# Five stage borders of a hybrid decoder step: stores, dilated pieces, one gate unit, waits per k-block, and a load in four parts

## The chip, the cores and the metric

The kernel runs on one core of a Trainium2 chip. The metric is the device time of one execution in microseconds; the figure for a kernel is the median of its runs. The profile is one execution recorded by the hardware profiler. Its engines are PE (TensorE, matmuls), PEld (its weight loads), DVE (VectorE), ACT (ScalarE), POOL (GpSimd) and SP (the sync engine, here only a queue that issues transfers). All of them run at once and are ordered by semaphores.

## The reference

One layer of a decoder for a prompt (256 tokens) and a sample group (8 sequences of 8 new tokens with 2048 past ones), 320 columns together. All data is 32-bit.

```python
h = rmsnorm(x, g_pre_mix)                              # 2048 channels
q_f, k_f, v_f, f_logit, q_d, k_d, v_d = split(h @ w_in)  # 8 fox heads, 3 x 4 dilated heads, 128 wide
o_fox = softmax(q k / sqrt(128) + forget_bias) v       # prompt: causal; sample: paged cache of 2048 keys
o_dil = three dilated windows (128,1) (512,4) (2048,16), merged by their softmax sums
g_fox, g_dil = split(sigmoid(h @ w_gate + b_gate))     # 2 x 2048 gates
m = (g_fox * (o_fox @ w_o_fox) + g_dil * (o_dil @ w_o_dil)) @ w_out
x1 = x + rmsnorm(m, g_post_mix)
y = x1 + rmsnorm(swiglu(rmsnorm(x1, g_pre_ffn), w_gate_up, w_down), g_post_ffn)   # 5632 wide
# also returned: y, new keys, values and log-forgets, and the shifted window caches
```

## The kernel before

**Units and panels.** Every dense product is made of units of 128 output columns. The weights of two units make a panel (2 MB) that SP loads into one of two slots of `raw`. ScalarE copies a unit's half into `w_hi` in a rounded format (`split_hi`, L1269; in the gate stage `gate_split`, L1369), VectorE computes the remainder `w_lo` (L1592, L1803), and TensorE runs three matmuls for each of the 16 k-blocks: `w_hi` by `act_hi`, `w_hi` by `act_lo`, `w_lo` by `act_hi`. Units are numbered: 0 to 23 fox queries, keys and values; 24 to 59 the dilated ones; 60 to 91 gates; 92 (`U_O`) to 107 the two attention output projections, twelve k-blocks each; 108 (`U_OUT`) to 123 the output projection; 124 on up and gate of the FFN, and 212 to 275 the down projection in four quarters of 11 k-blocks. Panel p holds units 2p and 2p + 1. Each engine runs its own program in written order; counting semaphores tie them: `unit_done` (TensorE has finished a unit), `hi_done`/`lo_done` (its weights are split), `acc_free` (its result has been taken from PSUM, unit u gives the value u + 3).

**Projections (to 585 us).** TensorE runs units 0 to 65. A natural-layout copy of keys goes through `k_stage` (two slots; `nat_rows`, L1313 on) and out by Pool's stores (L602, L603). ScalarE waits for `k_out` before it overwrites a slot. At units 10 to 14 the forget bias of the caches is computed (`fbx`), which Pool stores to `scratch_fb` (L595). Between half units, the attention of the prompt runs in pieces: half unit t = 2u or 2u + 1 starts a head's piece if `FOX_AT` or `DIL_AT` (L372) says so. A dilated head begins with its scores at t0; probabilities are normalised by VectorE at t0 + 1, transposed by TensorE at t0 + 3 and copied by ScalarE (`d_pt`, L1353), multiplied with the values at t0 + 5, and the result copied by VectorE (`pd_free`, L1782).

**Gates.** The gates of a unit are evicted by ScalarE (`gate_out`, L1361) into `gst`, two slots, and stored by SP to `scratch_gates` (`store_gates`, L483), since they are needed only at units 92 to 107. `gate_out(u)` waits until store u - 2 has landed. SP's program alternates stores and panels: ahead of panel p it stores the gates up to `due` (L494). From unit 66 on (`U_DEC`) all panels use slot 0 of `raw`, because slot 1's place holds value tiles.

**Attention of the samples (588 to 1285 us).** Nine blocks, one for each sequence and one more: block q works on the keys of sequence q and the values of sequence q - 1, tile by tile in 24 steps. Keys come through a ring of three buffers (`kraw`, L653) and values through one of four (`vraw`, L690), 512 KB a tile, both issued by Pool when TensorE has read a buffer. Before its first new key Pool waits for `pd_free` of all dilated heads, clears `fb` (L679) and loads the bias (L697). `GATE_UNITS` (L345) says how many gate units each block interleaves: (2, 3, 3, 3, 4, 3, 3, 3, 2), units 66 to 91. After the last block TensorE turns the last output (`turn_out`), VectorE takes it (`take_out`), ScalarE and VectorE split it into `o_hi` and `o_lo` (L1470, L1942; semaphore `o_sp`), and unit 92 starts.

**Output projections.** For each unit 92 to 107 VectorE first splits the unit after next (`step`), then multiplies with the gates `gl` and merges (`merge_trip`, L1945 on) into a k-block of `act_hi` and `act_lo`. TensorE waits for the last merge (`pe.wait_ge(acc_free, U_OUT + 2)`, L1192) before it starts unit 108.

**FFN and tail.** `x1`, the residual, was stored to scratch. Beside the FFN Pool copies the window caches (`copy_windows`, 22 pieces in 18 units, paced by `unit_done`), and between the copies of the seventh and the eighth sequence it loads `x1T` (2.5 MB, L774). VectorE needs it only at the very end.

Of the kernel before, what the change touches and what calls it, by code (L numbers as in the profile page):

```python
# [143 lines left out]
def build(nc, I, O, scratch):  # L144
    with ExitStack() as ctx:
# [199 lines left out]
        GATE_UNITS = (2, 3, 3, 3, 4, 3, 3, 3, 2)  # L345
# [26 lines left out]
        FOX_AT, DIL_AT = 50, (88, 94, 120, 126)  # L372
# [78 lines left out]
        def _(sp):  # L451
# [34 lines left out]
            for p in range(U_O // 2):  # L486
# [7 lines left out]
                due = 2 * p - (4 if p <= U_DEC // 2 else 2)  # L494
# [40 lines left out]
        def _(pool):  # L535
# [43 lines left out]
            for h in range(HG):  # L579
# [12 lines left out]
                                    bass.IndirectOffsetOnAxis(ap=tcol[:, 0:1], axis=0)).then_inc(lfp_ld, 16)  # L592
            pool.wait_ge(fbx_ok, 1)
# [3 lines left out]
            kp = O["fox_k_prompt"][0, 0].rearrange("(t p) h d -> p t (h d)", p=P)  # L597
            ks = O["fox_k_sample"][0].rearrange("b t h d -> (b t) (h d)")
            for i in range(4):
# [3 lines left out]
                pool.dma_start(ks[:, 256 * i:256 * i + 256], k_stage[0:NS, s, 2, :]).then_inc(k_out[s], 16)  # L603
# [119 lines left out]
            pool.wait_ge(g_st[1], 16 * KT)  # L723
# [35 lines left out]
            def copy_windows(b):  # L759
# [14 lines left out]
            pool.dma_start(x1T[:], scratch["x1T"].rearrange("k p t -> p k t")).then_inc(x1_ld, 16)  # L774
            copy_windows(DB - 1)
# [14 lines left out]
        def _(pe):  # L790
# [392 lines left out]
            turn_out(DB - 1)  # L1183


            pe.wait_ge(acc_free, U_O + 2)
# [941 lines left out]
```

## Time and profile before

| | us |
|---|---|
| median of 3 runs | 2504.24 |
| lowest, highest | 2496.71, 2505.09 |
| profiled execution, span (first to last instruction) | 2501.8 |
| TensorE busy in it | 2347.5 (94%) |
| VectorE, ScalarE, Pool busy | 1066.3, 811.7, 465.1 |
| transfers in it | 585.84 MB |

The page gives the profiled execution's span and no time around it; the median stands 2.4 us over that span. The busy shares are means over stages with different limits, so the stages have to be read one by one: in the timeline, a number in brackets at the end of a row is the time that the engine sat idle before the instruction, with what ended the wait.

### The profile page before, as it was taken

Reading aid. Unit: us, or ns where it says so; the run is one execution under the profiler, and the core shown is the slowest. Engines: PE = TensorE matmul, PEld = TensorE weight load, DVE = VectorE, ACT = ScalarE, POOL = GpSimd, SP = SyncE. Lnnn points to the kernel's source line nnn. Section 1 sums busy time; section 2 is a strip of 40 time slices with the busy share of each in tenths; the row PEclk is TensorE's granted clock in tenths of the full one; section 3 lists DMA queues with packets and bytes.
Section 4 is the critical chain, followed back from the end, with each engine's and each line's share of the span. In section 5 each row is a group of like instructions: output and inputs, shape, how many; then the busy total and the mean of one; then the engine's idle time right before and its main releaser. Section 6 shows DMA issues by size and latency. Waiting matters only on the chain.

```text
span 2501.8 us, 45253 instructions
## 1 busy us (share of the span) xinstructions
PE 2347.5 (94%) x18252; PEld 2140.3 (86%) x18252; DVE 1066.3 (43%) x1433; ACT 811.7 (32%) x982; POOL 465.1 (19%) x874
## 2 busy tenths in 40 slices
PE   7999999997899998999989896999999999999997
PEld 6999999996666666766659895999999999999997
DVE  6443443433333332333326436444444444444445
ACT  3223333332333333333312234232332332333234
POOL 2010000101333333333211232111111111111111
PEclk8999999998999999999989998999999999999998
DMA  8554344535899999999876544667676767688873
GB/s 250 159 153 150 119 144 130 185 125 172 283 348 354 338 314 348 349 343 320 318 242 193 177 157 146 226 230 238 230 247 220 256 217 247 221 276 280 289 272 101
DMA packets 340076, 585.84 MB, mean 234 GB/s; under 512 B 20575, under 2 KB 283043, under 8 KB 336255
## 3 DMA queue, kind: packets, MB, share of 16 engines
q0 software_dynamic: 70704, 309.02, 35.2%
q1 hardware_dynamic: 269232, 274.86, 34.7%
q8 instruction: 99, 1.62, 0.3%
q14 instruction: 41, 0.34, 0.0%
HBM read 564.06 MB, written 109.39 MB: 269 GB/s over the span
## 4 chain that ended last, share of the span: by engine, by line
PE 77%; DMA 11%; issue 4%; DVE 4%; ACT 2%; POOL 1%; POOLq 0%; SPq 0%; DVEq 0%; ACTq 0%
PE ps L798 14%; PE ps L800 14%; PE ps L799 14%; DMA kraw<-in_cache_fox_k 6%; PE ps L836 5%; PE ps L838 5%; PE ps L837 5%; PE ps L1025 3%; DMA kraw<-in_cache_win_k 2%; PE ps L1030 2%; PE ps L1050 2%; PE ps L1110 1%; PE ps L1014 1%; PE ps L1016 1%; PE ps L1015 1%
## 5 line engine op out<-in xcount | busy, mean ns | idle before, releaser
L1592 DVE TENSOR_TENSOR w_lo<-raw,w_hi 128x2048 fp32r<-128x2048 f32 (+2 forms) x250 | 525.6, 2102 | 813.5 <-ACT w_hi L1269 813.5
L1269 ACT ACTIVATE w_hi<-raw 128x2048 fp32r<-128x2048 f32 (+2 forms) x250 | 439.3, 1757 | 1058.0 <-PE ps L800 770.5
L798 PE MATMUL ps<-act_hi,w_hi 128*128 128x320 f32 x1632 | 507.1, 311 | 12.3 <-DVE act_lo L1956 6.6
L799 PE MATMUL ps<-act_lo,w_hi 128*128 128x320 f32 x1632 | 506.7, 310 | 0.0
L800 PE MATMUL ps<-act_hi,w_lo 128*128 128x320 f32 x1632 | 506.5, 310 | 0.0
L836 PE MATMUL ps<-act_hi,w_hi 128*128 128x320 f32 x1024 | 322.9, 315 | 3.2 <-DVE v_stage L1700 3.2
L798 PEld LDWEIGHTS ps<-act_hi,w_hi 128*128 128x128 f32 x1632 | 308.2, 189 | 12.8 <-DVE act_lo L1956 6.9
L838 PE MATMUL ps<-act_hi,w_lo 128*128 128x320 f32 x1024 | 316.9, 309 | 0.0
L837 PE MATMUL ps<-act_lo,w_hi 128*128 128x320 f32 x1024 | 316.7, 309 | 0.0
L799 PEld LDWEIGHTS ps<-act_lo,w_hi 128*128 128x128 f32 x1632 | 308.3, 189 | 0.0
L800 PEld LDWEIGHTS ps<-act_hi,w_lo 128*128 128x128 f32 x1632 | 308.2, 189 | 0.0
L1838 DVE COPY kT<-ps 128x512 f32<-128x512 f32 x176 | 121.5, 690 | 231.3 <-PE ps L1030 230.8
L1402 ACT ACTIVATE kT<-ps 128x512 f32<-128x512 f32 x184 | 109.5, 595 | 312.1 <-PE ps L1025 311.9
L836 PEld LDWEIGHTS ps<-act_hi,w_hi 128*128 128x128 f32 x1024 | 192.6, 188 | 4.3 <-DVE w_lo L1592 3.5
L837 PEld LDWEIGHTS ps<-act_lo,w_hi 128*128 128x128 f32 x1024 | 192.6, 188 | 0.1
L838 PEld LDWEIGHTS ps<-act_hi,w_lo 128*128 128x128 f32 x1024 | 192.3, 188 | 0.0
L1025 PEld LDWEIGHTS ps<-ident,kraw 128*128 128x128 f32 x736 | 80.1, 144 | 108.9 <-DMA kraw<-in_cache_fox_k 49.7
L767 POOL TENSOR_TENSOR tick<-tick 1x1 f32<-1x1 f32 x144 | 28.2, 196 | 723.5 <-PE ps L800 714.6
L1025 PE MATMUL ps<-ident,kraw 128*128 128x128 f32 x736 | 123.7, 292 | 33.8 <-DMA kraw<-in_cache_fox_k 26.3
L1014 PE MATMUL ps<-act_hi,w_hi 128*128 128x320 f32 x416 | 149.6, 360 | 0.0
L1015 PE MATMUL ps<-act_lo,w_hi 128*128 128x320 f32 x416 | 130.2, 313 | 0.0
L1016 PE MATMUL ps<-act_hi,w_lo 128*128 128x320 f32 x416 | 130.1, 313 | 0.0
(368 smaller groups left out, 3735.7 us busy)
## 6 DMA issues: line engine op xcount, KB each, us to landing
raw<-in_w_gate_up SPq DMA_DIRECT2D x88, 1024.0 KB, 6.4
kraw<-in_cache_fox_k POOLq DMA_DIRECT2D x128, 512.0 KB, 6.8
vraw<-in_cache_fox_v POOLq DMA_DIRECT2D x128, 512.0 KB, 7.6
raw<-in_w_in SPq DMA_DIRECT2D x60, 1024.0 KB, 7.8
raw<-in_w_gate SPq DMA_DIRECT2D x32, 1024.0 KB, 15.0
raw<-in_w_down SPq DMA_DIRECT2D x32, 1024.0 KB, 5.8
out_win_k_sample<-in_cache_win_k POOLq DMA_DIRECT2D x64, 510.0 KB, 5.9
out_win_v_sample<-in_cache_win_v POOLq DMA_DIRECT2D x64, 510.0 KB, 3.9
```

What stands on the lines that cost most here:

```text
L798: pe.matmul(ps[:, bk_, 0:T], w_hi[:, slot, k, :], xh[:, x_k, :], start=(k == k0), stop=False)
L799: pe.matmul(ps[:, bk_, 0:T], w_hi[:, slot, k, :], xl[:, x_k, :], start=False, stop=False)
L800: mm = pe.matmul(ps[:, bk_, 0:T], w_lo[:, slot, k, :], xh[:, x_k, :], start=False, stop=(k == k1 - 1))
L836: pe.matmul(acc, w_hi[:, u % 2, k, :], act_hi[:, k, :], start=(k == 0), stop=False)
L837: pe.matmul(acc, w_hi[:, u % 2, k, :], act_lo[:, k, :], start=False, stop=False)
L838: mm = pe.matmul(acc, w_lo[:, u % 2, k, :], act_hi[:, k, :], start=False, stop=(k == KT - 1))
L1014: pe.matmul(acc, w_hi[:, u % 2, k, :], act_hi[:, k, :], start=(k == 0), stop=False)
L1015: pe.matmul(acc, w_hi[:, u % 2, k, :], act_lo[:, k, :], start=False, stop=False)
L1016: mm = pe.matmul(acc, w_lo[:, u % 2, k, :], act_hi[:, k, :], start=False, stop=(k == KT - 1))
L1025: mm = pe.transpose(ps[:, 2, P * j:P * j + P], kraw[:, n % KRING, P * j:P * j + P], ident[:])
L1269: act.activation(w_hi[:, slot, 0:kt, :], raw[:, pslot, 0:kt, P * slot:P * slot + P], ACT.Copy).then_inc(hi_done, 1)
L1592: dve.tensor_tensor(w_lo[:, slot, 0:kt, :], raw[:, pslot, 0:kt, P * half:P * half + P], w_hi[:, slot, 0:kt, :].bitcast(F32), ALU.subtract) ...
```

## The change

Five places are edited.

1. *Key stores.* Pool stores the first two pairs of fox keys ahead of the wait for `fbx` and the stores of `scratch_fb`, and the other two behind them.
2. *Start of the attention.* The last two dilated heads begin a half unit earlier (`DIL_AT` 119 and 125). SP stores gates 62 and 63 ahead of panel 33 instead of behind it.
3. *End of the attention.* The last block interleaves one gate unit instead of two; unit 91 runs behind `turn_out`. ScalarE and VectorE split unit 92 first, take and split the last output, then evict unit 91 and split unit 93. SP issues panel 47 before the store of unit 91, and Pool waits for that store only before the last four loads of `gl`.
4. *Unit 108.* TensorE starts it when its weights are split and waits for the two last merges only at k-blocks 14 and 15. VectorE merges unit 107 before it splits unit 109.
5. *x1.* The load becomes four of 640 KB, placed before the second, 7th, 12th and 17th piece of the last sequence's window copies.

```diff
-        GATE_UNITS = (2, 3, 3, 3, 4, 3, 3, 3, 2)
+        GATE_UNITS = (2, 3, 3, 3, 4, 3, 3, 3, 1)
-        FOX_AT, DIL_AT = 50, (88, 94, 120, 126)
+        FOX_AT, DIL_AT = 50, (88, 94, 119, 125)
...
-                due = 2 * p - (4 if p <= U_DEC // 2 else 2)
+                due = 2 * p - (4 if p < U_DEC // 2 else 2)
...
-            store_gates(U_O - 2, U_O)
+            store_gates(U_O - 2, U_O - 1)
             sp.wait_ge(pv_done, DB * KPG)
             load_panel(1, U_O, [(0, wof[:, :, 256:512]), (8, wod[:, :, 256:512])])
+            store_gates(U_O - 1, U_O)
...
+            store_fox_keys(0)
+            store_fox_keys(1)
             pool.wait_ge(fbx_ok, 1)
             for b in range(DB):
                 pool.dma_start(fbd[b].rearrange("h (g t) -> g h t", t=P), fbx[NPG * b:NPG * b + NPG]).then_inc(fb_st, 16)
+            store_fox_keys(2)
+            store_fox_keys(3)
...
-            pool.wait_ge(g_st[1], 16 * KT)
+            pool.wait_ge(g_st[1], 16 * KT - 16)
...
-            with pool.Fori(0, KT // 4) as i:
+            with pool.Fori(0, KT // 4 - 1) as i:
                 for k in range(4):
-                    pool.wait_ge(acc_free, i * 4 + (U_O + k - 1))
-                    pool.dma_start(gl[:, k], halves[bass.ds(i * 4 + k, 1)].rearrange("e p o t -> p (e o) t")).then_inc(g_ld[k], 16)
+                    load_gates(i, k)
+            pool.wait_ge(g_st[1], 16 * KT)
+            for k in range(4):
+                load_gates(KT // 4 - 1, k)
...
+                    if m % 5 == 1 and m // 5 < quarters:
+                        part = slice(4 * (m // 5), 4 * (m // 5) + 4)
+                        pool.dma_start(x1T[:, part, :], scratch["x1T"][part].rearrange("k p t -> p k t")).then_inc(x1_ld, 16)
...
-            pool.dma_start(x1T[:], scratch["x1T"].rearrange("k p t -> p k t")).then_inc(x1_ld, 16)
-            copy_windows(DB - 1)
+            copy_windows(DB - 1, 4)
...
             turn_out(DB - 1)
-            pe.wait_ge(acc_free, U_O + 2)
+            dense(U_O - 1, 0, KT)
+            pe.wait_ge(acc_free, U_O + 1)
             pe.wait_ge(o_sp, 1)
...
-            pe.wait_ge(acc_free, U_OUT + 2)
-            for e in range(KT):
+            pe.wait_ge(lo_done, U_OUT + 1)
+            for k in range(KT):
+                if k >= KT - 2:
+                    pe.wait_ge(acc_free, U_O + k + 3)
+                acc = ps[:, 0, 0:T]
+                pe.matmul(acc, w_hi[:, 0, k, :], act_hi[:, k, :], start=(k == 0), stop=False)
+                pe.matmul(acc, w_hi[:, 0, k, :], act_lo[:, k, :], start=False, stop=False)
+                mm = pe.matmul(acc, w_lo[:, 0, k, :], act_hi[:, k, :], start=False, stop=(k == KT - 1))
+            mm.then_inc(unit_done, 1)
+            for e in range(1, KT):
...
+            def last_gate():
+                for late in range(2):
+                    gate_split(U_O, late)
+                act.wait_ge(o_ev, DB)
+                act.activation(o_hi[:, :, SEQ:T], o32[:, :, SEQ:T], ACT.Copy).then_inc(os_h, 1)
+                gate_out(U_O - 1)
+                for late in range(2):
+                    gate_split(U_O + 1, late)
...
-            for n in range(6):
-                gates_after(DB + 1, n)
+            for late in range(2):
+                gate_split(U_O, late)
             take_out(DB - 1)
             dve.wait_ge(os_h, 4)
             dve.tensor_tensor(o_lo[:, :, SEQ:T], o32[:, :, SEQ:T], o_hi[:, :, SEQ:T].bitcast(F32), ALU.subtract).then_inc(o_sp, 1)
+            for late in range(2):
+                gate_split(U_O + 1, late)
...
-                    step(i * 4 + (U_O + k), k, KT if last and k >= 2 else KO)
+                    if last and k == 3:
+                        dve.wait_ge(unit_done, U_OUT)
+                    else:
+                        step(i * 4 + (U_O + k), k, KT if last and k >= 2 else KO)
...
             merge_trip(KT // 4 - 1, True)
+            split_lo(1, 0, U_OUT + 1)
...
-            dve.wait_ge(x1_ld, 16)
+            dve.wait_ge(x1_ld, 64)
```

What stands in a row on the engines, at three of the places. In these rows a semaphore behind "waits" is one that the instruction waits for.

SP at the end of the projections, before: the panels 31 to 33 and the gate stores.

```order
L467 DMA raw<-in_w_gate 128x8x256 [waits lo_done]
L467 DMA raw<-in_w_gate 128x8x256
L483 DMA scratch_gates<-gst 128x320 [waits acc_free] x2
L467 DMA raw<-in_w_gate 128x8x256 [waits lo_done]
L467 DMA raw<-in_w_gate 128x8x256
L483 DMA scratch_gates<-gst 128x320 [waits acc_free] x4
```

And after:

```order
L467 DMA raw<-in_w_gate 128x8x256 [waits lo_done]
L467 DMA raw<-in_w_gate 128x8x256
L483 DMA scratch_gates<-gst 128x320 [waits acc_free] x4
L467 DMA raw<-in_w_gate 128x8x256 [waits lo_done]
L467 DMA raw<-in_w_gate 128x8x256
L483 DMA scratch_gates<-gst 128x320 [waits acc_free] x2
```

The stores of gates 62 and 63 moved from behind panel 33, the second pair of loads, to ahead of it.

ScalarE at the same place, before: the gate outputs (gst) of units 63, 64 and 65, the splits (w_hi) behind them, and the copy of the last dilated probabilities (d_pt).

```order
L1361 ACTIVATE gst<-ps,cols 128x320 [waits unit_done]
L1269 ACTIVATE w_hi<-raw 128x2048 [waits raw_ld0]
L1361 ACTIVATE gst<-ps,cols 128x320 [waits unit_done,g_st0,out_lf]
L1269 ACTIVATE w_hi<-raw 128x2048 [waits raw_ld0]
L1353 ACTIVATE d_pt_103<-ps 128x1152 [waits pd_t]
L1361 ACTIVATE gst<-ps,cols 128x320 [waits unit_done,g_st1,out_lf]
```

And after:

```order
L1387 ACTIVATE gst<-ps,cols 128x320 [waits unit_done]
L1295 ACTIVATE w_hi<-raw 128x2048 [waits raw_ld0]
L1379 ACTIVATE d_pt_103<-ps 128x1152 [waits pd_t]
L1387 ACTIVATE gst<-ps,cols 128x320 [waits unit_done,g_st0,out_lf]
L1295 ACTIVATE w_hi<-raw 128x2048 [waits raw_ld0]
L1387 ACTIVATE gst<-ps,cols 128x320 [waits unit_done,g_st1,out_lf]
```

The copy moved ahead of the gate output of unit 64 and of the split of unit 66.

TensorE behind the last attention block, before: the last turn of the output, then unit 92.

```order
L1144 MATMUL ps<-ident,of 128x128 [waits od_ok,of_ok]
L1144 MATMUL ps<-ident,of 128x128
L1146 MATMUL ps<-sel,od 128x16 x2
L1188 UNCONDITIONAL_BRANCH [waits o_sp,acc_free]
L1188 ISA
L798 MATMUL ps<-o_hi,w_hi 128x320 [waits acc_free,lo_done]
```

And after:

```order
L1161 MATMUL ps<-ident,of 128x128 [waits od_ok,of_ok]
L1161 MATMUL ps<-ident,of 128x128
L1163 MATMUL ps<-sel,od 128x16 x2
L853 MATMUL ps<-act_hi,w_hi 128x320 [waits acc_free,lo_done]
L854 MATMUL ps<-act_lo,w_hi 128x320
```

The 48 matmuls of gate unit 91 stand between the turn and the wait for `o_sp`.

VectorE at the last merge, before: the split of unit 109 (w_lo), then the merge of unit 107.

```order
L1592 TENSOR_TENSOR w_lo<-raw,w_hi 128x2048 [waits hi_done,unit_done]
L1952 TENSOR_TENSOR mtmp<-ps,gl 128x320 [waits g_ld3]
L1953 TENSOR_TENSOR mtmp<-ps,gl 128x320
L1954 TENSOR_TENSOR mtmp<-mtmp 128x320 [waits vchain]
L1955 CAST act_hi<-mtmp 128x320 [waits vchain]
L1956 TENSOR_TENSOR act_lo<-mtmp,act_hi 128x320 [waits vchain]
```

And after:

```order
L1991 TENSOR_TENSOR mtmp<-ps,gl 128x320 [waits g_ld3,unit_done]
L1992 TENSOR_TENSOR mtmp<-ps,gl 128x320
L1993 TENSOR_TENSOR mtmp<-mtmp 128x320 [waits vchain]
L1994 CAST act_hi<-mtmp 128x320 [waits vchain]
L1995 TENSOR_TENSOR act_lo<-mtmp,act_hi 128x320 [waits vchain]
L1626 TENSOR_TENSOR w_lo<-raw,w_hi 128x2048 [waits hi_done]
```

The split moved behind the merge.

## Rows read from the trace of the kernel before

**Rows 1.** The page, part 4: shares of the chain that ended last, by engine.

```profile
PE 77%; DMA 11%; issue 4%; DVE 4%; ACT 2%; POOL 1%; POOLq 0%; SPq 0%; DVEq 0%; ACTq 0%
```

**Rows 2.** Timeline, key stores: start, duration, engine, line, operation, [idle before <- releaser].

```profile
157.20 4.28 POOL L595 DMA_DIRECT2D scratch_fb<-fbx  x8 [68.91 <-DVE fbx L1744]
...
164.77 0.38 ACT L1325 ACTIVATE k_stage<-ps 128x256 f32<-128x256 f32 x1 [12.32 <-DMA out_fox_k_sample<-k_stage]
...
170.58 0.38 PE L836 MATMUL ps<-act_hi,w_hi 128*128 128x320 f32 x1 [3.22 <-DVE v_stage L1700]
```

**Rows 3.** Timeline, start of the samples' attention, all engines.

```profile
571.36 1.02 SPq L467 DMA_DIRECT2D raw<-in_w_gate  x2
572.42 13.13 SPq L483 DMA_DIRECT2D scratch_gates<-gst  x4
...
581.43 0.53 ACT L1361 ACTIVATE gst<-ps,cols 128x320 f32<-128x320 f32 x1 [12.50 <-DMA scratch_gates<-gst]
...
584.83 0.48 PE L991 MATMUL ps<-d_pt,dV 128*128 128x256 f32 x1 [3.95 <-ACT d_pt L1353]
...
588.13 1.04 PE L1025 MATMUL ps<-ident,kraw 128*128 128x128 f32 x4
...
589.31 0.42 DVE L1782 COPY o<-ps 128x256 f32<-128x256 f32 x1
...
605.53 0.69 PE L1025 MATMUL ps<-ident,kraw 128*128 128x128 f32 x2 [8.31 <-DMA kraw<-in_cache_fox_k]
```

**Rows 4.** Timeline, end of the attention.

```profile
1269.49 1.05 POOL L690 DMA_DIRECT2D vraw<-in_cache_win_v  x2 [2.10 <-PE ps L1116]
...
1275.87 1.05 PE L1116 MATMUL ps<-vraw,pg 128*16 128x256 f32 x8 [2.74 <-DMA vraw<-in_cache_win_v]
...
1291.15 0.61 PE L798 MATMUL ps<-o_hi,w_hi 128*128 128x320 f32 x1 [5.42 <-DVE o_lo L1942]
```

**Rows 5.** Timeline, between the two output projections.

```profile
1386.12 2.29 DVE L1592 TENSOR_TENSOR w_lo<-raw,w_hi 128x2048 fp32r<-128x2048 f32 x1 [0.77 <-ACT w_hi L1269]
...
1390.68 0.64 PE L798 MATMUL ps<-act_hi,w_hi 128*128 128x320 f32 x1 [6.61 <-DVE act_lo L1956]
...
1399.75 1.92 ACT L1269 ACTIVATE w_hi<-raw 128x2048 fp32r<-128x2048 f32 x1 [13.74 <-PE ps L800]
```

**Rows 6.** Timeline, down projection at the load of x1T.

```profile
2363.52 2.64 ACT L1269 ACTIVATE w_hi<-raw 128x1408 fp32r<-128x1408 f32 x2 [9.14 <-DMA raw<-in_w_down]
...
2367.09 0.60 PE L798 MATMUL ps<-q_hi,w_hi 128*128 128x320 f32 x1 [5.89 <-DVE yacc L2057]
...
2373.95 1.38 ACT L1269 ACTIVATE w_hi<-raw 128x1408 fp32r<-128x1408 f32 x1 [7.79 <-PE ps L800]
```

**Rows 7.** Stretches: from:to, length, busy (x) of each engine, PEclk, DMA share, GB/s.

```profile
571.40:579.60 8.20, 7.76 (x56) 7.50 (x55) 1.15 (x3) 0.00 (x0) 0.00 (x0) 1.00 0.90 288
...
592.30:605.50 13.20, 4.26 (x53) 3.18 (x53) 2.46 (x10) 0.60 (x1) 3.96 (x7) 0.76 1.04 253
...
1391.00:1400.00 9.00, 9.00 (x52) 9.00 (x52) 0.00 (x0) 0.25 (x1) 1.08 (x1) 0.80 1.07 365
...
1560.00:1800.00 240.00, 240.00 (x1639) 240.00 (x1638) 109.88 (x102) 73.10 (x52) 27.71 (x76) 1.00 0.69 231
```

**Rows 8.** The page, part 6: transfers, KB each, median us from issue to landing.

```profile
raw<-in_w_down SPq DMA_DIRECT2D x32, 384.0 KB, 7.2
...
x1T<-scratch_x1T POOLq DMA_DIRECT2D x1, 2560.0 KB, 13.6
```

**Rows 9.** The chain in order of time: start, us, what.

```profile
813.59 1.71 POOL fb L697 x3
...
893.08 1.71 POOL fb L697 x3
...
980.99 1.71 POOL fb L697 x3
...
2345.71 17.78 DMA raw<-in_w_down
```

More of the change, by code:

```diff
@@ L592, in _, with store_fox_keys @@
                                     bass.IndirectOffsetOnAxis(ap=tcol[:, 0:1], axis=0)).then_inc(lfp_ld, 16)
-            pool.wait_ge(fbx_ok, 1)
-            for b in range(DB):
-                pool.dma_start(fbd[b].rearrange("h (g t) -> g h t", t=P), fbx[NPG * b:NPG * b + NPG]).then_inc(fb_st, 16)
             kp = O["fox_k_prompt"][0, 0].rearrange("(t p) h d -> p t (h d)", p=P)
             ks = O["fox_k_sample"][0].rearrange("b t h d -> (b t) (h d)")
-            for i in range(4):
+            def store_fox_keys(i):
                 s = i % 2
@@ L603, in _ @@
                 pool.dma_start(ks[:, 256 * i:256 * i + 256], k_stage[0:NS, s, 2, :]).then_inc(k_out[s], 16)
+            store_fox_keys(0)
+            store_fox_keys(1)
+            pool.wait_ge(fbx_ok, 1)
+            for b in range(DB):
+                pool.dma_start(fbd[b].rearrange("h (g t) -> g h t", t=P), fbx[NPG * b:NPG * b + NPG]).then_inc(fb_st, 16)
+            store_fox_keys(2)
+            store_fox_keys(3)
             pool.wait_ge(nat_ev, 2 * HF)
@@ L726, in _, with load_gates @@
             halves = gsc.rearrange("(o e) p t -> e p o t", o=2)
-            with pool.Fori(0, KT // 4) as i:
+            def load_gates(i, k):
+                pool.wait_ge(acc_free, i * 4 + (U_O + k - 1))
+                pool.dma_start(gl[:, k], halves[bass.ds(i * 4 + k, 1)].rearrange("e p o t -> p (e o) t")).then_inc(g_ld[k], 16)
+            with pool.Fori(0, KT // 4 - 1) as i:
                 for k in range(4):
-                    pool.wait_ge(acc_free, i * 4 + (U_O + k - 1))
-                    pool.dma_start(gl[:, k], halves[bass.ds(i * 4 + k, 1)].rearrange("e p o t -> p (e o) t")).then_inc(g_ld[k], 16)
+                    load_gates(i, k)
+            pool.wait_ge(g_st[1], 16 * KT)
+            for k in range(4):
+                load_gates(KT // 4 - 1, k)
             pool.wait_ge(acc_free, U_OUT + 2)
@@ L757, in _, with copy_windows @@
             pool.wait_ge(tick_ok, 1)
-            def copy_windows(b):
+            def copy_windows(b, quarters=0):
                 for m, (g, x, n, rows) in enumerate(pieces):
                     unit = m * 18 // len(pieces)
+                    if m % 5 == 1 and m // 5 < quarters:
+                        part = slice(4 * (m // 5), 4 * (m // 5) + 4)
+                        pool.dma_start(x1T[:, part, :], scratch["x1T"][part].rearrange("k p t -> p k t")).then_inc(x1_ld, 16)
                     if m == 0 or unit != (m - 1) * 18 // len(pieces):
@@ L1466, in _ @@
             sequence(DB, None, DB - 1)
-            for n in range(6):
-                gates_after(DB + 1, n)
-            act.wait_ge(o_ev, DB)
-            act.activation(o_hi[:, :, SEQ:T], o32[:, :, SEQ:T], ACT.Copy).then_inc(os_h, 1)
+            gate_out(U_O - 2)
+            last_gate()
             ahead[:] = [panel_landed(U_O // 2) - loads(U_O) - 32, panel_landed(U_O // 2 + 1) - loads(U_O) - 32]
@@ L1937, in _ @@
             sequence(DB, None, DB - 1)
-            for n in range(6):
-                gates_after(DB + 1, n)
+            for late in range(2):
+                gate_split(U_O, late)
             take_out(DB - 1)
```

## The prediction

> **What bounds the kernel now.** I read the page first: the chain that ended last is TensorE for 77% of the span and transfers for 11% [rows 1]. A change can win only where TensorE waits on that chain, or where its clock is down because it waited. So I went through TensorE's timeline for waits, and took clock and transfers from the stretches view. The attention (606 to 1284 us) is largely paced by key and value transfers, and the change leaves its inner order alone. Outside it there are few long waits, and the change addresses five places: 3.22 us before 170.58 [rows 2], 3.95 and 8.31 at the start of the attention [rows 3], 5.42 at its end [rows 4], 6.61 between the two output projections [rows 5], 5.89 in the last quarter of the down projection [rows 6].
>
> A unit is one 128-column block of weights, 16 k-blocks of three matmuls. In a stretch without waits 1639 matmuls take 240 us [rows 7], 0.1464 us each, so a unit takes 7.03 us, and a down unit (11 k-blocks) 4.83. After the waits of 6.61 and 5.89 us the engine is slow for a while: the unit from 1390.68 to 1399.75 took 9.07 us instead of 7.03 [rows 5], and the granted clock of that stretch is 0.80 of 2.4 GHz [rows 7], a mix of 1.2 and 2.4. The down unit from 2367.09 to 2373.95 took 6.86 instead of 4.83 [rows 6]. So a long wait costs its length and 2.0 us more. The 3.22 us wait started no such phase: its first matmul takes 0.38 us, against 0.60 to 0.64 after the long ones [rows 2, 5, 6].
>
> **Key stores first (border 1).** Pool waits for fbx, issues the eight stores of scratch_fb at 157.20 for 4.28 us, and only then the key stores. ScalarE wants to overwrite k_stage, sits 12.32 us until a key store has landed, the next weight split behind it is late, and TensorE waits 3.22 us [rows 2]. With the first two pairs of key stores ahead of the wait for fbx they land before ScalarE asks. The scratch_fb stores keep their time; what now waits behind them is the third pair, whose tile is written only then. Gain 3.2 us. Nothing is late next: the weight panels are not waited for here. The bounds are 0 and 3.2; I take 3.2, since the named releaser is the very thing moved.
>
> **Dilated pieces and gate stores (border 2).** Now the sync queue issues panel 33 at 571.36 and behind its wait the stores of gate outputs 62 to 65. ScalarE may not overwrite gst before store 62 has landed and sits 12.50 us, to 581.43. Its copy of the last dilated probabilities comes after that, so TensorE waits 3.95 us, from 580.9, and does the last product slowly, to 588.13. VectorE copies the result at 589.31, which lets Pool clear fb, load it and fetch the next keys, and TensorE waits for these to 605.53 [rows 3].
> After the change stores 62 and 63 go out before panel 33, as soon as their outputs are written, and the gst wait goes. Late next is panel 33 itself. From 571.4 to 579.6 the transfers move 8.2 x 288 GB/s = 2.36 MB [rows 7], the panel's 2.10 and some gate outputs, so it lands by 579.6. ScalarE's split of unit 66 (1.9 us) ends at 581.5, VectorE's (2.3 us) at 583.9, and in VectorE's order the copy that frees Pool comes then: 584.3 instead of 589.7, **5.4 us** earlier. If the keys land as long after it as now, the gain is 5.4. The other bound is panel 34, issued when VectorE has split unit 67, now just ahead of that copy at 589.4. TensorE's unit 65 will end at about 582 (580.9, and about 1.5 for the product at full clock, done inside it); 0.5 us of eviction and 1.9 and 2.3 of splits put the issue at 587.1, only **2.3 us** earlier. Now fb and keys start 3 us behind the panel, then they start with it, and the engines are full from 592.3 to 605.5 at only 253 GB/s [rows 7]. If that whole backlog ends last, the gain is 2.3. I take the middle, 3.9 us, as no row is nearer to one end.
> The Trainium skill, page "DMA: Bandwidth & Descriptors", section "Queues, rings and completion order", says that a DMA engine takes turns between its queues packet by packet. By that rule Pool's key load shares the engines with the panel until the panel is through, the lower bound holds, and the sum comes out 1.6 us less. The trace shows only the case with the panel ahead and does not settle it.
>
> **A gate unit behind the attention (border 3).** Now TensorE waits 5.42 us behind the last attention output [rows 4] and starts the output projection slowly, 2.0 us more by the price above. Unit 91 (7.03 us) takes this place and hides the eviction of unit 90, the splits of unit 92 and the copy and low part of o, that 5.4 us in all. Its own eviction and the splits of unit 93 (about 4 us) hide under unit 92 (12 k-blocks, 5.3 us). At the border alone that is 5.42 + 2.0 - 7.03 = 0.4 us. The rest is how much shorter the last attention block gets without the unit, between 0 (value transfers pace it) and 7.03 (TensorE paces it). There are four value buffers, and a load starts when its buffer is read; the pair issued at 1269.49 is used from 1275.87 [rows 4]: 6.4 us, or 1.6 us a value tile, while TensorE's work per tile is 32/24 of a k-block (0.44 us) and 0.5 for the values (1.05 at half clock), 1.1 us. So much of the block is paced by transfers and saves nothing. TensorE paces its end, from 1275.87 on, at half clock at first [rows 4]: some 3 of its gate steps go there, 2.5 us; I put another 1.5 on the rest. I take 4.0, so border 3 gives **4.4 us**, with 0.4 and 7.4 as ends.
>
> **Waits per k-block (border 4).** Now VectorE first splits unit 109 (1386.12, 2.29 us) and then merges the last output unit, 2.3 us to 1390.68, and TensorE waits 6.61 us, from 1384.07 [rows 5]. After the change VectorE merges first, to about 1386.5, and TensorE works through 14 k-blocks of unit 108 (6.2 us, to 1390.2) before it needs the last two. The split of unit 109 moves behind the merge and ends at 1388.9, before unit 108 does at 1391.1, so the removed wait has no successor. Unit 108 ends at 1391.1 instead of 1399.75: **8.6 us**. Pool's load of xT starts with the merge and meets panel 56: 4.7 MB together, 12.9 us at the 365 GB/s of [rows 7], so by 1400; the first split of that panel is due after unit 110, at 1405. The bounds are 6.6 (the slow phase stays) and 8.7.
>
> **x1 in four parts (border 5).** Now x1T, 2.5 MB, goes out just ahead of a down panel, which is then 17.78 us on its way from 2345.71 [rows 9]; ScalarE waits 9.14 us for it, to 2363.52, and TensorE 5.89 [rows 6]. TensorE's wait began at 2361.2, one unit after 2356.4, when the panel was due: it had 10.7 us. Its second part usually takes 7.2 us, and a quarter of x1T's 13.6 is 3.4 [rows 8]: 10.6 us if the quarter stood wholly ahead. It goes out behind the panel instead, and the others 4, 9 and 13 units later, so no wait. Gain 5.89 + 2.0 = **7.9 us**, the lower end 3 (one quarter still makes a panel a few us late). VectorE's wait for all four parts comes tens of us after the last.
>
> **The sum.** 3.2 + 3.9 + 4.4 + 8.6 + 7.9 = **28.0 us**. The profiled execution has a span of 2501.8 us and the median is 2504.24; the 2.4 us between them the change does not touch. 2504.24 - 28.0 = **2476.2 us**, 1.1% less. The lower ends of the five terms give 12.3, the upper ones 32.6.
>
> **Rivals.**
> (a) *The transfers hold borders 2 and 3.* The keys give 2.3 us and the last block nothing. For it: full engines from 592 to 605 [rows 7], a wait for values at 1275.87 [rows 4]. Against it: from there on TensorE is busy without a wait. 2504.2 - (3.2 + 2.3 + 0.4 + 8.6 + 7.9) = 2481.8.
> (b) *The x1 stall moves and does not go.* A quarter meets window pieces and a panel four times; 10.6 against 10.7 us leaves no room [rows 8]. One late panel brings back up to 7.9: 2484.1.
> (c) *The attention slips against its own panels*, slower than before. Its blocks start at 813.59, 893.08 and 980.99 [rows 9]: 79.5 us with three gate units, 87.9 with four. The change starts the attention with panel 34 and the keys at once. If that puts each later panel in front of the keys, and each of the six later blocks with three units takes what the one with four does, that is 6 x 8.4 = 50 us: 2526. It decides the sign from 4.7 us a block on. Against it: every block is re-ordered by its own waits, and the order inside is the same.
> (d) *The last block is TensorE's after all*, and the keys give 5.4: 1.5 + 3.0 more, 2471.7.
>
> **Chances.** Forecast 0.61, (a) 0.14, (b) 0.08, (c) 0.04, (d) 0.08, and 0.05 for most terms at their lower ends at once (12.3 us, 2491.9). A measurement of this kernel can tell about 0.5%, 12.5 us, from no change; the runs of before lie within 8.4. Forecast, (a), (b) and (d) all stay under 2491.7, which is the border of faster; the lower ends together are "same". The range goes from 2468 (below (d) by half the spread of the runs) to 2488 (above (b) by as much). Faster 0.91, same 0.05, slower 0.04.
>
> **What the profile after would show.** Border 1: no wait of ScalarE for out_fox_k_sample, none of TensorE over 1 us near 170. Border 2: gate output 64 near 570 in place of 581.43, ScalarE's next wait on raw, and the wait for keys ending near 598. Border 3: matmuls of act_hi between the last turn and the output projection, and no wait over 1 us there. Border 4: no wait of 6.61, and unit 108 in 7.0 us at clock 1.00. Border 5: four x1T loads, no wait of ScalarE on in_w_down over 1 us. I am wrong if a wait over 3 us stands at one of the last three borders, or if the attention, from its first waited key to its last value, is 5 us longer than the terms allow.

## The result, and the profile after

| | before | changed |
|---|---|---|
| median, us | 2504.66 (4 runs) | 2481.32 (4 runs, 2477.52 to 2485.61) |
| ratio, 95% interval | | 0.9910 (0.9897 to 0.9923) |
| five more runs of the changed kernel (e5 below) | 2504.69 (11 runs) | 2480.54, ratio 0.9902 (0.9889 to 0.9916) |
| span of the profiled execution | 2501.8 | 2482.7 |

The change takes 23.3 us off the median, 24.2 in the second comparison; the forecast was 28.0. By the intervals of the ratios it is 19 to 26 us and 21 to 28, so the 28.0 lies at or just beyond their upper ends. The time lies inside the predicted range (2468 to 2488) and 5.1 us above the predicted value. The two profiled spans differ by 19.1 only; 3.3 us of what is missing there is a stall that the profile of after shown here caught and other executions don't have (border 5 below). One run of e2 below took 5137.37 us; it counts in no ratio, and without it that median is 2502.55.

The chain that ended last, by engine, in the page of after:

```profile
PE 79%; DMA 11%; issue 4%; DVE 3%; ACT 2%; POOL 1%; POOLq 0%; SPq 0%; DVEq 0%; ACTq 0%
```

TensorE's share has risen by 2 points against [rows 1] and the transfers' 11% have not moved. That is a first hint, and no more: what was recovered is TensorE's waits at borders, and little of what transfers hold.

**Border 1.** Timeline of after, Pool (start, duration, engine, line, operation, [idle before <- releaser]):

```profile
131.07 0.79 POOL L601 DMA_DIRECT2D out_fox_k_prompt<-k_stage  x1 [42.57 <-ACT k_stage L1352]
...
146.03 0.73 POOL L601 DMA_DIRECT2D out_fox_k_prompt<-k_stage  x1 [13.62 <-ACT k_stage L1352]
...
157.41 2.68 POOL L608 DMA_DIRECT2D scratch_fb<-fbx  x5 [10.11 <-DVE fbx L1778]
```

The two key stores now go out 11 and 26 us ahead of the bias stores, which keep their time (157.20 in [rows 2]). ScalarE's wait for a key store and TensorE's 3.22 us are gone.

**Border 2.** Timeline of after, sync queue, ScalarE, VectorE and TensorE at the start of the attention:

```profile
563.90 0.33 SPq L483 DMA_DIRECT2D scratch_gates<-gst  x1
568.10 1.02 SPq L467 DMA_DIRECT2D raw<-in_w_gate  x2
...
570.10 0.53 ACT L1387 ACTIVATE gst<-ps,cols 128x320 f32<-128x320 f32 x1 [2.52 <-PE ps L855]
577.43 1.92 ACT L1295 ACTIVATE w_hi<-raw 128x2048 fp32r<-128x2048 f32 x1 [6.80 <-DMA raw<-in_w_gate]
...
581.66 0.42 DVE L1816 COPY o<-ps 128x256 f32<-128x256 f32 x1
...
584.30 1.02 SPq L467 DMA_DIRECT2D raw<-in_w_gate  x2
...
600.94 1.11 PE L1042 MATMUL ps<-ident,kraw 128*128 128x128 f32 x4 [7.31 <-DMA kraw<-in_cache_fox_k]
```

To be read against [rows 3]: gate output 64 comes at 570.10 instead of 581.43, then ScalarE waits for panel 33, as forecast. VectorE's copy, which frees Pool, comes at 581.66 instead of 589.31, 7.65 us earlier; 3.26 of these are border 1's, so 4.4 are left. But the keys arrive at 600.94 instead of 605.53, 4.59 earlier, so 1.3 without border 1. Panel 34 goes out at 584.30, in the middle of it. The chain in order of time (start, us from issue to landing) has the load of the first waited keys, in before, in after and in e12 below, where panel 34 goes out behind it:

```profile
595.34 10.15 DMA kraw<-in_cache_fox_k
```

```profile
587.67 13.23 DMA kraw<-in_cache_fox_k
```

```profile
588.72 9.09 DMA kraw<-in_cache_fox_k
```

The load goes out 4.4 us earlier in after (border 1 apart) and takes 3.1 us longer.

**Border 3.** TensorE and VectorE at the end of the attention, after:

```profile
1275.45 0.62 PE L1133 MATMUL ps<-vraw,pg 128*16 128x256 f32 x8 [1.26 <-DMA vraw<-in_cache_win_v]
...
1279.45 0.39 PE L853 MATMUL ps<-act_hi,w_hi 128*128 128x320 f32 x1
...
1283.48 0.96 DVE L1976 TENSOR_TENSOR o_lo<-o,o_hi 128x768 fp32r<-128x768 f32 x1 [0.91 <-ACT o_hi L1466]
```

Unit 91 starts at 1279.45 right behind the turn, and `o_lo` is written at 1283.48 beside it. The wait of 5.42 us in [rows 4] has no successor.

**Border 4.** VectorE's split of unit 109 in the timeline of after, and the stretch in which TensorE runs unit 108 (from:to, length, busy time and instructions of PE, PEld, DVE, ACT, POOL, PEclk, DMA share, GB/s):

```profile
1386.51 2.29 DVE L1626 TENSOR_TENSOR w_lo<-raw,w_hi 128x2048 fp32r<-128x2048 f32 x1 [3.39 <-ACT w_hi L1295]
```

```profile
1375.00:1386.00 11.00, 11.00 (x77) 11.00 (x76) 7.91 (x12) 3.43 (x2) 1.16 (x1) 1.00 0.48 149
```

TensorE is busy for the whole 11 us, at the full clock, where [rows 5] and the third stretch of [rows 7] had a wait of 6.61 and a clock of 0.80.

**Border 5.** Pool's four loads, ScalarE and TensorE, after:

```profile
2334.12 0.82 POOL L779 DMA_DIRECT2D x1T<-scratch_x1T  x1
...
2352.98 0.80 POOL L779 DMA_DIRECT2D x1T<-scratch_x1T  x1
...
2372.34 0.80 POOL L779 DMA_DIRECT2D x1T<-scratch_x1T  x1
...
2384.75 2.79 ACT L1295 ACTIVATE w_hi<-raw 128x1408 fp32r<-128x1408 f32 x2 [6.88 <-DMA raw<-in_w_down]
...
2388.42 0.38 PE L815 MATMUL ps<-a_hi,w_hi 128*128 128x320 f32 x1 [2.29 <-DVE yacc L2097]
```

Three of the four loads are shown; the fourth goes out at 2394.23. The first two pass unnoticed. Behind the third, ScalarE waits 6.88 us for a down panel and TensorE 2.29, where [rows 6] had 9.14 and 5.89.

### The profile page after: what moved, and what is told of

Its sections match the earlier page's. It is cut to its first block, busy times and chain, and to the rows that moved or that the text cites. A ratio compares the mean times of both kernels' runs of the same rounds, so it can differ in the third digit from the quotient of the medians.

```text
span 2482.7 us, 45242 instructions
## 1 busy us (share of the span) xinstructions
PE 2348.4 (95%) x18252; PEld 2140.8 (86%) x18252; DVE 1065.7 (43%) x1433; ACT 812.7 (33%) x982; POOL 468.8 (19%) x877
## 4 chain that ended last, share of the span: by engine, by line
PE 79%; DMA 11%; issue 4%; DVE 3%; ACT 2%; POOL 1%; POOLq 0%; SPq 0%; DVEq 0%; ACTq 0%
PE ps L815 14%; PE ps L817 14%; PE ps L816 14%; DMA kraw<-in_cache_fox_k 6%; PE ps L853 6%; PE ps L855 6%; PE ps L854 6%; PE ps L1042 3%; PE ps L1047 2%; DMA kraw<-in_cache_win_k 2%; PE ps L1067 2%; PE ps L1127 1%; PE ps L1031 1%; PE ps L1033 1%; PE ps L1032 1%
```

## The experiments

The theory from this comparison: borders 1 and 4 give what they should; border 2's lead is cut by panel 34 and then given back inside the attention, because transfers and not TensorE set its length; border 5 keeps a stall in some executions. In the expectations this theory is T, and T2 in its later form. The rivals: the forecast's terms all hold and the trace of after is a poor sample; or the attention absorbs whatever is done at its ends. Each edit was run alone on the kernel before or taken out of the changed one, and each suspected cause was changed by itself.

**e1: border 2 alone.**

```diff
-        FOX_AT, DIL_AT = 50, (88, 94, 120, 126)
+        FOX_AT, DIL_AT = 50, (88, 94, 119, 125)
...
-                due = 2 * p - (4 if p <= U_DEC // 2 else 2)
+                due = 2 * p - (4 if p < U_DEC // 2 else 2)
```

> The kernel before with the second edit alone (dilated pieces a half unit earlier, gates 62 and 63 stored ahead of panel 33). Theory T (each term is what the trace of after shows at its border, and the missing gain went there): the wait for the first keys ends only 1.3 to 1.6 us earlier, since their load now shares the transfer engines with panel 34, and the median falls by 1.5 us. Rival N (the trace of after is one execution among many; the forecast's term holds): 3.9 us. Rival A (the attention takes back any earlier start, because its blocks run against transfers that the start doesn't move): the keys 1.5 or more earlier, but no gain is left at the last value of the attention, 0 us. T and A differ in the lead at block 8: more than 1 us by T, none by A.

Measured: 2502.13 against 2505.90, ratio 0.9984 (0.9969 to 0.9999), which is 0.3 to 7.8 us: T's 1.5 and N's 3.9 are both inside, rival A's 0 just outside. In the traces (table below) the keys come 2.0 us earlier than in before, and block 8 begins no earlier (879.33 against 879.02), as rival A has it; one pair of traces can't settle it.

**e2: border 3 alone** (the hunks of the third edit; the first of them):

```diff
-        GATE_UNITS = (2, 3, 3, 3, 4, 3, 3, 3, 2)
+        GATE_UNITS = (2, 3, 3, 3, 4, 3, 3, 3, 1)
...
             turn_out(DB - 1)
+            dense(U_O - 1, 0, KT)
```

> The kernel before with the third edit alone (one gate unit moved behind the attention). Theory T: the last block 4.5 us shorter and no wait over 1 us behind it, 5.3 us in all. Rival N: the forecast's 4.4 us. Rival A (the last block is shorter in after only because the attention arrived there with another lead): the block is shorter by 2 us or less here and the edit gives 1 to 3 us.

Measured: 2502.80 against 2505.90, ratio 0.9994 (0.9980 to 1.0008), at most 5.0 us. T's 5.3 us is just outside; N's 4.4 and A's 1 to 3 are both inside.

**e3: border 5 alone.**

```diff
-            pool.dma_start(x1T[:], scratch["x1T"].rearrange("k p t -> p k t")).then_inc(x1_ld, 16)
-            copy_windows(DB - 1)
+            copy_windows(DB - 1, 4)
...
```

> The kernel before with the fifth edit alone (x1T in four parts). Theory T: the third part meets a panel and window pieces, ScalarE waits some 7 us for that panel and TensorE about 2.3, so 5.3 us of the forecast's 7.9 are left. Rival N: no wait of TensorE over 1 us in the last quarter of the down projection, 7.9 us.

Measured: 2500.20 against 2505.90, ratio 0.9979 (0.9967 to 0.9991), 2.3 to 8.3 us. The trace has no wait of TensorE over 1 us in the last quarter: for this execution rival N is right.

**e4: the four parts at the tail**, on the changed kernel, behind the last window copy:

```diff
-            copy_windows(DB - 1, 4)
+            copy_windows(DB - 1)
...
+            for q, u in enumerate((269, 271, 273, 274)):
+                part = slice(4 * q, 4 * q + 4)
+                pool.wait_ge(unit_done, u)
+                pool.dma_start(x1T[:, part, :], scratch["x1T"][part].rearrange("k p t -> p k t")).then_inc(x1_ld, 16)
```

> The changed kernel with the four parts of x1T moved behind the last window copy, each behind a unit of the down projection (units 269, 271, 273 and 274 done). Theory T: TensorE's wait of 2.3 us in the last quarter goes and nothing takes its place, so 2.5 us less than the changed kernel, 25.8 less than the one before (2478.8). Rival P (the panels of that stretch are late by the window copies, x1T or not): the wait of 2.3 us stays, the time is that of the changed kernel, 2481.3. Rival L (the last part lands after VectorE wants it at the norm, 2463.5 in the profile of after): 2 to 10 us more than the changed kernel.

Measured: 2479.41 (2478.39 to 2481.61), ratio to before 0.9901 (0.9879 to 0.9922). No stall (rival P falls), and VectorE does not wait at the norm (rival L falls).

**e5: the changed kernel once more**, with no edit.

> The changed kernel once more, unaltered, with a second profile. Theory V (the shortfall of the last term is one of single executions: the third part of x1T makes a panel late in some of them and not in others): the runs fall in two groups, near 2478 and near 2485 as the four so far, and this profile has either the wait of 2.3 us in the last quarter of the down projection or none. Rival F (the wait is there in every execution): the profile has it again, and the runs lie in one group. In both the median is 2481.3 within 2.

Measured: 2480.54 (2477.15 to 2483.36). Two rows of the sync queue and of Pool at the third part:

```profile
2366.17 1.00 SPq L467 DMA_DIRECT2D raw<-in_w_down  x2
```

```profile
2368.50 0.80 POOL L779 DMA_DIRECT2D x1T<-scratch_x1T  x1
```

The panel goes out 2.3 us ahead of the third part, exactly as in the first profile (2370.01 and 2372.34), but no engine waits for it over 1 us: the later of its two loads took 14.1 us to land there and 6.0 here. V's single executions are right. Its two groups of runs are not: the five lie anywhere between 2477 and 2484. In the profile with the stall the panels' loads were slow before the third part went out, too (8.7 to 9.8 us for the later load of the four panels ahead of it, 5.9 to 8.1 here), so that part is not shown to be the cause. Why the same order of transfers makes a panel late once and not at other times stays open.

**e6: the changed kernel without border 2** (the two lines of e1 undone).

> The changed kernel with the second edit undone (pieces and gate stores at the start of the attention as before). Theory T2 (the attention is held by its transfers, and a lead at its start is given back by its last block): no or little loss, 0 to 1.5 us more than the changed kernel, and the last value of the attention comes as early as in it, within 1.5 us. Rival N (the forecast's term): 3.9 us more, all of it still there at the last value.

Measured: 2482.10, 1.6 us above e5 (ratios to before 0.9905 and 0.9902, each ±0.0015 or 4 us). That is on T2's side, but does not exclude N's 3.9.

**e7: the changed kernel without border 3.**

> The changed kernel with the third edit undone (both gate units in the last block, none behind the attention). Theory T2: the last block is shorter by little in the changed kernel, since its values arrive no earlier, so undoing it costs 1 to 2.5 us. Rival N: 4.4 us. Rival D (the last block is TensorE's): 5.3 to 7.4 us.

Measured: 2488.33 (2484.70 to 2491.37), ratio 0.9931 (0.9918 to 0.9944), 7.8 above e5. T2's 1 to 2.5 us is missed; the median is nearest to rival D. The wait is back:

```profile
1288.89 0.60 PE L807 MATMUL ps<-o_hi,w_hi 128*128 128x320 f32 x1 [5.42 <-DVE o_lo L1959]
```

**e8: shorter gate panels in the attention.** Seven of the 16 k-blocks of these panels are not loaded, and the units multiply with older weights there; every instruction still runs.

```diff
-                load_panel(..., [(0, cols_of(w, c, 0, 8)), (8, cols_of(w, c, 8, KT))])
+                load_panel(..., [(0, cols_of(w, c, 0, 8)), (8, cols_of(w, c, 8, 9 if p > U_DEC // 2 else KT))])
```

> The changed kernel with gate panels 34 to 45 loaded to 9 of 16 k-blocks; the other 7 are left out, so those gate units multiply with older weights, and the number of instructions on every engine stays the same. 12 panels times 0.92 MB make 11.0 MB less between the first keys and the last values. Theory T2 (transfers hold the attention, at 325 GB/s): the attention is 25 to 34 us shorter. Rival E (TensorE and the handshakes hold it): under 5 us shorter. Between, 5 to 25, it would be held by both in turn.

Measured: 2448.93, ratio 0.9771 (0.9750 to 0.9792), 31.6 us less than e5. All engines in the stretch from 735 to 1233 us, of the changed kernel and of e8:

```profile
735.00:1233.00 498.00, 456.77 (x4943) 329.63 (x4942) 171.79 (x375) 175.22 (x305) 163.05 (x306) 0.97 0.96 337
```

```profile
735.00:1233.00 498.00, 467.79 (x5142) 330.67 (x5143) 177.83 (x382) 179.59 (x313) 170.32 (x322) 0.99 0.95 336
```

The engines move 337 and 336 GB/s: taking bytes away leaves the rate as it was and lets more matmuls (5142 against 4943) into the same time. Cut at the same two events, the last new values of the first block and those ahead of the last one, e5 and e8 do the same work:

```profile
728.53:1227.85 499.32, 460.06 (x5002) 332.32 (x4998) 173.16 (x380) 175.21 (x305) 162.47 (x306) 0.97 0.96 338
```

```profile
726.34:1196.04 469.70, 448.55 (x5003) 323.91 (x4999) 173.33 (x380) 175.28 (x305) 162.62 (x306) 1.00 0.96 340
```

Of the 29.6 us between them, 18.1 are time in which TensorE had no matmul (39.3 against 21.2), and 11.5 are shorter matmuls, at a granted clock of 1.00 instead of 0.97. From the first waited key to the last new values it is 676.3 us in the changed kernel, 674.8 in e5 and 645.2 in e8. 31.6 us for 11.0 MB is 2.9 us per MB, and 1 MB at 337 GB/s is 3.0 us. Transfers set the length of the attention; rival E falls.

**e9: border 1 alone** (`store_fox_keys(0)` and `(1)` ahead of the wait for `fbx_ok`).

```diff
+            store_fox_keys(0)
+            store_fox_keys(1)
             pool.wait_ge(fbx_ok, 1)
...
```

> The kernel before with the first edit alone (key stores ahead of the forget bias). Theory S (behind the wait a slow phase of TensorE's clock begins in some executions: in four traces that have the wait, 3.5, 3.5, 5.0 and 6.1 us are lost there): the trace has 3.5 us less than the one of before between the 16th and the 24th split of weights and the median falls by 4.5. Rival N (no slow phase, as the forecast had it): 3.2 us.

Measured: 2499.56 against 2505.08, ratio 0.9978 (0.9969 to 0.9987): 5.5 us (3.3 to 7.8).

**e10: border 4 alone** (its hunks in TensorE's and VectorE's programs).

```diff
-            pe.wait_ge(acc_free, U_OUT + 2)
+            pe.wait_ge(lo_done, U_OUT + 1)
...
+                if k >= KT - 2:
+                    pe.wait_ge(acc_free, U_O + k + 3)
```

> The kernel before with the fourth edit alone (waits per k-block in unit 108). All theories: 8.6 us less between units 107 and 109, as in six traces that have the edit, and 8.6 us less in the median. Rival M (part of it comes back where TensorE next waits, at the start of the FFN): 8.6 at the border, and 1.5 us or more of it lost by the first up unit, so 6 to 7 us in the median.

Measured: 2495.97 against 2505.08, ratio 0.9959 (0.9945 to 0.9973): 9.1 us, by the ratio 10.3. Nothing is lost at the start of the FFN: from the split of unit 113 to that of unit 129 it is 144.7 us here and 145.5 in before.

**e11: borders 2 and 3 together** on the kernel before (the edits of e1 and e2).

> The kernel before with the second and the third edit, the two whose terms rest on the attention. Theory T2 (transfers hold the attention; the start gives nothing that lasts and the unit 2.7 us, as the traces so far have it on the mean): 1 to 5 us less. Rival N (the forecast's terms): 8.3 us less.

Measured: 2502.95 against 2505.08, ratio 0.9996 (0.9985 to 1.0008). The two terms that rest on the attention are worth 2.1 us in the median and at most 3.8 by the interval, not 8.3. This is the experiment that tells T2 from N.

**e12: panel 34 behind the keys**, on the kernel of e4:

```diff
+                if p == U_DEC // 2 + 1:
+                    sp.wait_ge(k_ld[0], 32)
                 load_panel(raw_slot(p), ...)
```

> The changed kernel with the four parts of x1T at the tail (as in e4_x1_tail) and with panel 34 issued only when the first waited keys have landed. Theory P (panel 34 beside the keys is what holds them): the wait for the first keys ends 2 to 4 us earlier than in the changed kernel, measured from the end of the projections. Rival Q (the keys' own load, with the bias and three tiles, takes that long): under 1 us earlier. By T2 (transfers hold the attention) neither changes the end: the median is that of e4_x1_tail, 2479.4, within 2; by N it is earlier by what the keys are, 2 to 4 us.

Measured: 2479.54 (2478.31 to 2481.99). Sync queue and TensorE in its trace:

```profile
597.82 1.02 SPq L467 DMA_DIRECT2D raw<-in_w_gate  x2
```

```profile
597.85 1.11 PE L1048 MATMUL ps<-ident,kraw 128*128 128x128 f32 x4 [3.18 <-DMA kraw<-in_cache_fox_k]
```

TensorE's wait for the first keys is 3.18 us long instead of 7.31. P is right about the keys, which come 4.2 us earlier than in e4 by the table, and T2 about the end: the median is e4's within 0.2 us. With four runs each the two medians are uncertain by 2 to 3 us, so a small part of the lead may be left, but not all of it.

**All traces side by side.** Medians of single edits are blurred by 2 to 4 us, but the traces can be cut at fixed events. The stretches, from starts in each timeline: *B1* from ScalarE's split of unit 16 to that of unit 24; *keys* from the split of unit 40 to the end of the wait for the first keys; *block 1 ends* from the same split to the start of that block's last new values (735.00 in before); *block 8 begins* to the last new values ahead of the last block (1233.27 in before); *unit 97* from the same split to the split of unit 97; *B4* from the split of unit 105 to that of unit 113; *end* from a split in the down projection (2332.20 in before, 2318.41 in after) to the end of the span. For before, 214.73 - 150.54 = 64.19, and so on.

| trace | edits | B1 | keys | block 1 ends | block 8 begins | unit 97 | B4 | end |
|---|---|---|---|---|---|---|---|---|
| before | - | 64.19 | 251.28 | 380.75 | 879.02 | 961.22 | 59.50 | 169.60 |
| e3 | 5 | 63.98 | 252.02 | 380.74 | 877.22 | 957.92 | 59.39 | 161.38 |
| e9 | 1 | 60.72 | 251.76 | 381.96 | 881.36 | 960.64 | 59.81 | 169.51 |
| e10 | 4 | 65.83 | 251.47 | 382.35 | 883.09 | 962.12 | 50.89 | 169.05 |
| e2 | 3 | 65.71 | 251.15 | 380.65 | 878.97 | 957.70 | 60.03 | 169.62 |
| e6 | 1 3 4 5 | 60.72 | 251.45 | 378.93 | 878.36 | 956.25 | 50.89 | 161.03 |
| e1 | 2 | 66.87 | 249.24 | 378.09 | 879.33 | 956.41 | 59.22 | 169.31 |
| e7 | 1 2 4 5 | 60.71 | 249.24 | 379.91 | 880.10 | 961.03 | 50.89 | 161.30 |
| e11 | 2 3 | 65.94 | 248.91 | 379.27 | 879.04 | 956.47 | 60.21 | 169.57 |
| after | all | 60.72 | 249.95 | 379.88 | 880.96 | 957.82 | 50.89 | 164.29 |
| e5 | all | 60.71 | 249.21 | 377.66 | 876.98 | 955.57 | 50.90 | 161.03 |
| e4 | all, x1 at tail | 60.72 | 249.90 | 379.80 | 877.84 | 954.98 | 50.89 | 161.00 |
| e12 | e4, panel 34 late | 60.72 | 245.74 | 377.34 | 877.52 | 954.44 | 50.90 | 161.00 |
| e8 | all, short panels | 60.72 | 246.64 | 374.52 | 844.22 | 923.38 | 50.89 | 161.82 |

Columns B1 and B4 repeat to 0.01 us where their waits are gone, and column end to 0.8, but for one stall. The attention does not: with the same code around it block 8 is reached with a scatter (standard deviation) of 1.5 to 2 us, and that scatter is why means over traces are used below.

## Why the prediction was nearly right, and where its terms were wrong

**Border 1, forecast 3.2, measured 4.7.** Column B1 has a mean of 65.4 in the six traces with the wait and 60.7 in all the others. The removed wait is 3.0 to 3.5 us long each time; what the forecast missed is the slow phase of TensorE's clock behind it. I had read its absence off one execution, from a first matmul of 0.38 us. The stretch just behind, for before, e1 and e2:

```profile
166.00:176.00 10.00, 6.78 (x48) 6.53 (x47) 5.76 (x6) 3.83 (x6) 1.27 (x2) 1.00 0.64 199
```

```profile
166.00:176.00 10.00, 6.85 (x31) 6.61 (x30) 5.75 (x6) 3.70 (x6) 1.27 (x2) 0.69 0.67 206
```

```profile
166.00:176.00 10.00, 6.78 (x37) 6.54 (x36) 5.75 (x6) 3.69 (x6) 1.27 (x2) 0.83 0.67 201
```

The granted clock is 1.00 in the first, 0.69 and 0.83 (a mix of 1.2 and 2.4 GHz) in the others, and the time lost goes with it: 3.5, 6.2 and 5.0 us over the 60.7. e2's first matmul behind the wait also took 0.39 us, so that sign was worth nothing. In before itself the loss was 3.5: the forecast was right for the one execution it was read from. Rival N in e9 (3.2 us) lies just outside the interval (3.3 to 7.8).

**Border 2, forecast 3.9 (2.3 to 5.4), measured 2.1 at the keys and about 1.4 behind the attention.** Up to the keys the working held at its lower bound: column keys is 251.5 without the edit (six traces, scatter 0.3) and 249.4 with it (six, scatter 0.4; e12 and e8 left out). The step that failed is the choice of the middle. Panel 34 beside the keys was the named cause of the lower bound, and e12 shows it by taking the panel away: 245.7, so 5.8 us earlier than without the edit, the upper bound of 5.4 and a little more (e8, with a panel 34 of little over half the size, stands between at 246.6). The bound itself was put a little high: VectorE's copy came 4.4 us earlier and not 5.4, as panel 33 took 9.3 us from its issue at 568.10 to ScalarE's split at 577.43, and not 8.2. In e12 the key load is 1.1 us shorter than in before, too (9.09 against 10.15). The rule of the Trainium skill that the prediction cited ("DMA: Bandwidth & Descriptors", "Queues, rings and completion order") put the sum 1.6 us lower. The trace agrees with it as far as the bound goes: with the panel issued 3.4 us ahead of the key load, the load takes 13.23 us instead of 9.09. How the engines divide their time between the two no run here shows.
The step that was missing comes behind: a lead at the start of the attention does not last. With the edit block 1 ends 1.8 us earlier (379.1 against 380.9), block 8 begins 0.6 earlier (879.0 against 879.7), and at unit 97 there are 1.1 and 1.75 us in the two pairs of groups (with border 3, e12 counted in, and without). The first is uncertain by 1.4 us and the others by 2, so they alone don't show that anything is lost behind the keys, and e1's median (0.3 to 7.8) would fit the full 3.9. What shows it is e12 against e4: of 4.2 us more lead at the keys, 2.5 are left at the end of block 1 (377.34 against 379.80), 0.3 at block 8 and 0.5 at unit 97, and the medians agree; and e11, which bounds borders 2 and 3 together. The forecast took over a gain at the first keys to the end; e8 says why that can't be done: the transfers run at 337 GB/s from there on, and a TensorE that is early waits for them.

**Border 3, forecast 4.4 (0.4 to 7.4), measured 2 to 3.** The wait of 5.42 us went and nothing followed, as worked out. At unit 97 the edit is worth 2.9 us in the traces with border 2 (958.7 to 955.9) and 3.5 in those without (960.5 to 957.0), uncertain by 2 to 3, as groups of two to five traces scatter by 1 to 3 us. The stretch from block 8 to unit 97, the difference of two columns, leaves out what comes ahead of the last block: 79.9 us in the six traces without the edit, 77.7 in the seven with it (e8 left out), so 2.2 us, uncertain by 1.7. By these two the term was too high by 1 to 2, and the likely part is the one put at 4.0, how much shorter the last block gets: TensorE still waits for value tiles in it (1.26 us at 1275.45 above). No run measures that part by itself. The medians don't narrow it down: 3.1 alone (1.5 by the ratio), 7.8 taken out of the changed kernel, each uncertain by 3 to 5; rival D (5.3 to 7.4) can't be excluded from e7 alone, while e2, e11 and the traces speak against it.

**Border 4, forecast 8.6, measured 8.8.** Column B4 is 50.9 with the edit in eight traces and 59.2 to 60.2 without, 59.7 on the mean. Wait and slow phase both went, as priced, and the split of unit 109 was never waited for.

**Border 5, forecast 7.9, measured 7.6.** Column end falls from a mean of 169.4 to 161.8 in six traces: 8 us or more in four of them, 7.6 in e8, and 5.2 in the one with the stall. So rival (b), the stall that moves, exists, but as one execution in six and worth 3 us, not 7.9. With the parts at the tail (e4, e12) the column is 161.00 twice and the eight runs lie between 2478.3 and 2482.0, against 2477.2 to 2485.6 for nine of the changed kernel. The medians, 2479.4 and 2479.5 against 2481.3 and 2480.5, are no measurable gain.

**The sum.** 4.7 + 1.4 + 3.2 + 8.8 + 7.6 = 25.7 us from the traces, 23.3 and 24.2 in the medians: they agree within the 3 us of the intervals. The medians leave 2.2 and 3.1 us for borders 2 and 3 together once the other three are taken off, as e11 does (2.1), where the traces at unit 97 have 4.6. Against 28.0 the attention's two terms are 3.7 short and border 1 is 1.5 over: that the total came so near is in part luck, since these errors have opposite signs. Rival (a), the transfers hold borders 2 and 3, named 2481.8 and comes nearest to the 2481.3; its mechanism is the right one for border 2, and for border 3 it went too far (0.4 against 2 to 3). Rival (c) didn't come: the changed attention needs 676.3 us from key to last values, [rows 3] and the last new values of before (1283.05) make 677.5. Rival (d) falls: the keys gave 2.1 us and not 5.4, and the last block went on waiting for values.

Of the marks set beforehand, gate output 64, ScalarE's wait on `raw`, border 3 and border 4 came as written; the keys at 598 (they came at 600.94) and no wait of ScalarE over 1 us at x1T did not.

## What to carry to other kernels

Before a gain at the start of a stage is added to the sum, ask what paces the stage behind it: if a stretch view shows the transfer engines nearly always busy (here a share of 0.96 at 337 GB/s for 500 us) while TensorE has no matmul for 8% of it, a head start is worth little, and a megabyte less (2.9 us here) is what counts. When an edit brings one transfer forward, look for what else its semaphores release in the same microsecond, and take the bound that shares the engines. Behind a wait of some 3 us the slow clock phase came in four traces of six: price it by its mean over executions, not by the one in the profile.

## What the runs showed of the hardware that was not expected

Behind the same wait of 3.0 to 3.5 us TensorE's granted clock over ten microseconds was 1.00 in two traces (before, e3), 0.83 in three (e2, e10, e11) and 0.69 in one (e1), with up to 2.7 us lost against before, without any difference in the program up to there. The length of the wait doesn't tell them apart: it was 3.22 us in before (1.00) and in e2 (0.83), and 3.15 in e1. The long stretch from the first up units to the down projection (1552.60 to 2318.41 in after), without a wait, took 765.81 or 765.82 us in every one of the fourteen traces. The stretch from the split of unit 24 to that of unit 40 took 139.51 or 139.52 us in all fourteen. So the spread of several microseconds between executions of this kernel comes from stretches that hold waits: besides the attention, from the start to the split of unit 16 (150.4 to 151.9 us) and from the split of unit 113 to that of unit 129 (144.7 to 147.0).
